# A two-layer diffusion trunk step: the first layer begins by channel blocks, the two empty token columns are dropped, and a gate product stands between each pair of preparation steps

## What is computed

```python
mod = silu(cond) @ w_ada + b_ada                  # cond: c_ctx for context tokens, c for latent tokens
sh1, sc1, g1, sh2, sc2, g2 = split(mod, 6)
h = rms(x, g_norm1) * (1 + sc1) + sh1
u = h @ w_in                                      # 1024 x 5728: 4096 gate columns, then the mixers' inputs
gates, xa, qkv_da, xc, mla_in = split(u)
# four mixers: pooling (xa), differential attention (q, k, v), Fourier (xc), latent attention (cq, ckv)
proj = einsum('btnw,nwd->btnd', branches, w_branch)
x = x + g1 * (sum(sigmoid(gates) * proj) @ w_out)
h2 = rms(x, g_norm2) * (1 + sc2) + sh2
u = h2 @ w_up                                     # 1024 x 5632
u = u[t-1] * conv_w[0] + u[t] * conv_w[1] + u[t+1] * conv_w[2] + conv_b    # within each token group
x = x + g2 * ((silu(gate) * val) @ w_down)        # 2816 x 1024
```

## Time and profile before

| | |
|---|---|
| median of 3 runs | 1329.32 us (1328.96 to 1331.95) |
| the profiled execution, its own time | 1332.93 us |
| its span in the trace | 1331.1 us |
| PE busy | 1290.0 us, 97% of the span |
| DVE busy, ACT busy | 750.8 us (56%), 599.5 us (45%) |
| moved by DMA | 198.05 MB, mean 149 GB/s |
| start of the first stream product | 42.08 us |

### The profile page before, as it was taken

One profiled execution on the slowest core, in us unless ns is written; L12 is line 12 of the kernel. 1 busy time (PEld: TensorE's weight loads), 2 busy tenths in 40 slices (PEclk: granted clock), 3 DMA queues, 4 the chain that ended last, 5 costly groups with the idle time before them and its releaser, 6 DMA issues.

```text
span 1331.1 us, 19314 instructions
## 1 busy us (share of the span) xinstructions
PE 1290.0 (97%) x7808; PEld 1194.1 (90%) x7808; DVE 750.8 (56%) x1292; ACT 599.5 (45%) x1000; POOL 85.3 (6%) x77
## 2 busy tenths in 40 slices
PE   4799999999999999999999999999999999999999
PEld 1796888889989999999989879898899899999998
DVE  0526258544858766673344542874476777777532
ACT  2445555453345544452244554555433655544321
POOL 1000000001810000000000000000053000000000
PEclk9799999999999999999999999999999999999999
DMA  9532144543463444447554312433436333333433
GB/s 365 213 113 88 64 175 143 188 145 123 163 221 112 143 144 153 148 142 258 201 194 162 119 64 73 142 135 133 168 111 222 111 127 127 122 120 123 136 133 127
DMA packets 53544, 198.05 MB, mean 149 GB/s; under 512 B 6416, under 2 KB 6832, under 8 KB 52944
## 3 DMA queue, kind: packets, MB, share of 16 engines
q1 hardware_dynamic: 53136, 196.13, 42.2%
q0 software_dynamic: 320, 0.69, 0.2%
HBM read 194.52 MB, written 2.27 MB: 148 GB/s over the span
## 4 chain that ended last, share of the span: by engine, by line
PE 88%; DVE 5%; issue 2%; SPq 1%; ACT 1%; DMA 1%; POOL 1%; DVEq 0%; POOLq 0%; ACTq 0%
PE bank L1161 25%; PE bank L1163 25%; PE bank L1162 25%; PE bank L1119 2%; PE bank L1373 2%; DVE wide L1035 1%; DMA w_raw<-stream 1%; DVE w_lo L797 1%; PE bank L1403 1%; PE bank L1383 1%; SPq L327 1%; PE bank L1374 1%; PE bank L1347 1%; PE bank L1371 1%; PE bank L1267 0%
## 5 line engine op out<-in xcount | busy, mean ns | idle before, releaser
L1161 PE MATMUL bank<-act_hi,w_hi 128*128 128x386 f32 x1424 | 493.8, 347 | 12.7 <-DVE act_lo L857 12.3
L1163 PE MATMUL bank<-act_hi,w_lo 128*128 128x386 f32 x1424 | 483.0, 339 | 0.0
L1162 PE MATMUL bank<-act_lo,w_hi 128*128 128x386 f32 x1392 | 472.7, 340 | 0.0
L797 DVE TENSOR_TENSOR w_lo<-w_raw,w_hi 128x1024 fp32r<-128x1024 f32 x258 | 317.8, 1232 | 268.8 <-ACT w_hi L489 268.5
L489 ACT ACTIVATE w_hi<-w_raw 128x1024 fp32r<-128x1024 f32 x258 | 270.9, 1051 | 169.0 <-DMA w_raw<-stream 169.0
L1161 PEld LDWEIGHTS bank<-act_hi,w_hi 128*128 128x128 f32 x1424 | 269.8, 189 | 21.3 <-issue 19.8
L1163 PEld LDWEIGHTS bank<-act_hi,w_lo 128*128 128x128 f32 x1424 | 269.5, 189 | 0.0
L1162 PEld LDWEIGHTS bank<-act_lo,w_hi 128*128 128x128 f32 x1392 | 263.9, 190 | 1.3
L1161 PE MATMUL bank<-mlp_hi,w_hi 128*128 128x386 f32 x352 | 120.0, 341 | 0.0
L1162 PE MATMUL bank<-mlp_lo,w_hi 128*128 128x386 f32 x352 | 119.1, 338 | 0.0
L1163 PE MATMUL bank<-mlp_hi,w_lo 128*128 128x386 f32 x352 | 118.9, 338 | 0.0
(11 more groups left out here) (204 smaller groups left out, 1431.6 us busy)
## 6 DMA issues: line engine op xcount, KB each, us to landing
w_raw<-stream SPq DMA_DIRECT2D x258, 512.0 KB, 3.7
ada<-ada_w SPq DMA_DIRECT2D x58, 512.0 KB, 3.7
ada_head_a<-ada_w SPq DMA_DIRECT2D x16, 512.0 KB, 6.3
ada_norm<-ada_w SPq DMA_DIRECT2D x16, 512.0 KB, 5.3
time_consts<-time_consts SPq DMA_DIRECT2D x2, 1920.0 KB, 15.5
ada_head_b<-ada_w SPq DMA_DIRECT2D x6, 512.0 KB, 15.4
params<-params SPq DMA_DIRECT2D x2, 926.0 KB, 11.3
x<-x_in SPq DMA_DIRECT2D x1, 1544.0 KB, 10.6
```

Of the source, the lines that this page charges most:

```text
L797: V.tensor_tensor(wlo[s][:, :], raw[s][:, :], whi[s][:, :].bitcast(F32), ALU.subtract).then_inc(lo_ready, 1)
L1161: T.matmul(out, wb[s][0][:, w, :], hi[k], start=first and k == 0, stop=False)
L1162: T.matmul(out, wb[s][0][:, w, :], lo[k], start=False, stop=False)
L1163: ins = T.matmul(out, wb[s][1][:, w, :], hi[k], start=False, stop=last and k == n - 1)
```

## The change

Three things are changed.

First, GAP is gone: TOK is 384 instead of 386, and everything that was 386 columns wide is 384. The memsets of the empty columns are gone too. Each outer tap of the convolution is made by two instructions, one for each token group (127 and 255 columns), instead of one of 385.

Second, layer 0 begins by channel blocks. w_ada's first two chunks come as 8 blocks of 1 MB, block j with the shift and scale of channel block j only; the first 7 stream units (`SKIP = 7`) come as 8 blocks of 448 KB (128 x 896 numbers), block j with their rows for channel block j. PE makes the modulation of a block with 32 matmuls of 64 moving columns (`start_modulate`) in place of 8 of 256 for the same data, and, when the block's activations are there, the products of that block with all 7 units into 7 banks (`start_products`, 21 matmuls). The squares are shared by ACT and DVE, and PE sums all 8 blocks with 8 matmuls instead of POOL's adds and 3 matmuls. x is loaded first, in two halves.

```diff
-SKIP = 0
+SKIP = 7
...
-MIX = ["xa0", "xa1", "q0", "q1", "k0", "k1", "v0", "v1", "xc0", "xc1", "cq", "ckv", "cqr"]
+MIX = ["xa0", "xa1", "q0", "q1", "k0", "k1", "xc0", "xc1", "v0", "v1", "cq", "ckv", "cqr"]
...
+            for h in range(2):
+                c0, c1 = h * KD // 2 * TOK, (h + 1) * KD // 2 * TOK
+                sp.dma_start(x_t[:, c0:c1], x_in[:, c0:c1]).then_inc(x_loaded[h], 16)
...
+            for j in range(KD):
+                if j >= START_ADA:
+                    sp.wait_ge(ada_done, 2 * (j - START_ADA + 1))
+                sp.dma_start(start_ada_buf[j % START_ADA][:, :], start_ada[j:j + 1, :, :].rearrange("a p n -> (a p) n")
+                             ).then_inc(start_ada_loaded[j % START_ADA], 16)
+                sp.dma_start(start_raw[j][:, :], start_w[j:j + 1, :, :].rearrange("a p n -> (a p) n")
+                             ).then_inc(start_w_loaded[j], 16)
...
+                def start_norm(j):
+
+                    c0 = j * 2 * STRIP
+                    turned_block = rt_t[:, c0:c0 + 2 * STRIP].rearrange("p (b c) -> p b c", c=STRIP)
+                    dve.wait_ge(ada_done, 2 * (j + 1))
+                    turn = V.transpose(rt_t[:, c0:c0 + 2 * STRIP], bank[7][:, c0:c0 + 2 * STRIP])
...
+                    if j == 0:
+                        start_low(0)
+                    own.wait()
+                    dve.wait_ge(rstd_ready, 1)
...
+                def start_squares():
+
+                    for k in range(KD):
+                        if k % 2 == 0:
+                            pe.wait_ge((start_sq_act, start_sq_dve)[k // 2 % 2], k // 4 + 1)
+                        ins = T.matmul(bank[4][:, 0:TOK], cc("ones"), wide[:, k, :], start=k == 0, stop=k == KD - 1)
+                    ins.then_inc(ss_done, 1)
+
+                def start_modulate(j):
+
+                    w = start_ada_buf[j % START_ADA]
+                    pe.wait_ge(start_ada_loaded[j % START_ADA], 16 * (j // START_ADA + 1))
+                    if j >= 1:
+                        pe.wait_ge(start_read, j)
+                    n = 2 * STRIP
+                    for k in range(KD):
+                        for strip in range(4):
+                            p0, c = STRIP * strip, (k * 4 + strip) * n
+                            ins = T.matmul(bank[7][p0:p0 + STRIP, j * n:(j + 1) * n], conds[:, k, :], w[:, c:c + n],
+                                           start=k == 0, stop=k == KD - 1)
+                    ins.then_inc(ada_done, 2)
+
+                def start_products(j):
+
+                    pe.wait_ge(start_w_lo, j + 1)
+                    pe.wait_ge(norm_lo, j + 1)
+                    for u in range(SKIP):
+                        out = bank[u][:, 0:TOK]
+                        wh, wl = start_hi[j][:, u * P:(u + 1) * P], start_lo[j][:, u * P:(u + 1) * P]
+                        T.matmul(out, wh, HI[j], start=j == 0, stop=False)
+                        T.matmul(out, wh, LO[j], start=False, stop=False)
+                        ins = T.matmul(out, wl, HI[j], start=False, stop=j == KD - 1)
...
+                    start_squares()
+                    start_modulate(0)
+                    start_modulate(1)
+                    for j in range(KD):
+                        start_products(j)
+                        if j + 2 < KD:
+                            start_modulate(j + 2)
```

Third, in both layers' preparation a gate product is taken before the first sums of squares, so that gates 0 to 5 stand one step earlier, and the Fourier products come before the pooling products:

```diff
+
+                gate(0)
 
                 pe.wait_ge(mod_read, FROM + 6 * l + 2 + l)
                 pe.wait_ge(psq, l * 7 + 7)
                 T.matmul(bank[6][:, 0:TOK], cc("ones"), wide[:, 4, :], start=True, stop=False)
                 T.matmul(bank[6][:, 0:TOK], cc("ones", 0, NOPE), wide[0:NOPE, 6, :], start=False, stop=True).then_inc(pss, 1)
                 T.matmul(bank[7][:, 0:TOK], cc("ones"), wide[:, 5, :], start=True, stop=True).then_inc(pss, 1)
-                gate(0)
+                gate(1)
...
-                gate(4)
                 gate(5)
```

305 lines of the change are left out of this document (175 added, 130 removed).

## The result

The changed kernel takes a median of 1299.62 us (1297.97 to 1300.75, 4 runs), the kernel before, run beside it, 1329.22. The ratio is 0.9767, with a 95% interval of 0.9752 to 0.9783: 29 to 33 us less. The profiled execution took 1300.75 us with a span of 1299.0, where the one before took 1332.93 with a span of 1331.1.

A forecast was written before the change was run, and what follows sets the result against it. PE, busy 97% of the span, was taken as the bound. Columns 5.7, preparation 4.7 and start 9.8 us sum to 20.2, from the median 1329.3 to 1309 us, with a range of 1301 to 1319.

The forecast's parts named there:

- Term 1: All products: dropping the two empty columns shortens 6,000 matmuls and the float32 sums, 5.7 us in all.
- so two columns less are 0.92 ns: Price of a matmul: 0.46 ns for each column and nothing fixed, read from products of 256 and 386 columns.
- The convolution in two pieces: w_up's taps on DVE: 0.8 us more for two units, covered by DVE's idle 2.2 to 3.0 us; cost 0.
- Term 2: Preparation: gate products placed between its steps cover PE's waits before L1258 and L1267 in both layers, 4.7 us.
- PE waits in three places only: After the start, once a layer: 1.8 us at the merge, 1.2 before L1258, 1.1 before L1267.
- Term 3: Start of layer 0 by channel blocks: seven units through at 64.8 us instead of 74.6, gain 9.8 us, bounds 1 to 18.
- I take 2.1, the middle: Start: modulation of one block, 64 records of 64 columns, put at 2.1 us between bounds of 0.86 and 3.4.
- short matmuls are nearly free: Rival for the start: loads hide and columns decide, start gains 15 to 18 us, 1301 to 1304 us; chance 0.12.
- the bound below: Start: modulation of a block priced by columns alone, 0.86 us; the start would then gain 18 us.
- PE cools in the start: Rival: PE waits about 2 us before product 0, the clock falls, costing 2.4 us, so 1312 us; chance 0.06.
- The merge is not touched: Merge: PE's wait for w_lo, 1.8 us once in a layer, was taken to stay as it is.

The follow-up runs named there:

- e1: Kernel before with only the 384 columns, no gap memsets and the two-piece convolution; old preparation and start: 1319.97 us, ratio 0.9935.
- e4: Changed kernel with 15 rows of 42 products appended, varying width and block stride: 384 columns 173.4 to 175.7 ns, 352 columns 161.2, 400 columns 182.1.
- e9: Kernel before, still 386 columns, with every tile behind act_lo moved up by 384 bytes: 1324.72 us, ratio 0.9961.
- e8: Kernel before, still 386 columns, with every tile behind act_lo moved up by 64 bytes: 1329.46 us, ratio 0.9992.
- e3: Changed kernel with the blocks of the two activation tiles 386 columns apart, products still 384 wide: 1301.10 us, ratio 0.9779.
- e6: Changed kernel with every tile behind act_lo moved up by 128 bytes: 1306.04 us, ratio 0.9801.
- e7: Changed kernel with every tile behind act_lo moved up by 64 bytes: 1299.88 us, ratio 0.9768.
- e14: Changed kernel with every tile behind act_lo moved up by 256 bytes: 1298.35 us, ratio 0.9750.
- e2: Kernel before with 384 columns and the new preparation (a gate product between each pair of steps), old start: 1313.68 us, ratio 0.9871.
- e12: Changed kernel with the start's modulation products of blocks 2 to 7 made twice: 1310.18 us, ratio 0.9847.
- e10: Changed kernel with four float32 products, result unread, filling PE's wait before the start's first product: 1298.19 us, ratio 0.9755.
- e13: Changed kernel with 21 rows of 42 products appended, weights fixed, moving block 0 to 1024 bytes further: 173.1 to 176.9 ns at 384 columns.
- e5: Changed kernel with 21 rows of 42 products appended, moving block and weights at chosen places: 173.3 to 175.7 ns at 384 columns.

## Why the prediction was right or wrong

**Term 1, columns: mis-sized, and the step that put the time outside the range.** 5.7 forecast, 9 (ratio) to 12.7 (traces) measured in e1. The step that failed is "so two columns less are 0.92 ns", which took for granted that a spacing depends on columns alone. The mean spacing of the products on the activations fell by 3.4 ns, from 177.1 to 173.7 (13.8 us over some 4,060 of them), that on the merged blocks by 3.7 ns (1.3 us), and w_down's gave 1.1 us: over 16 us. Of this 2.9 us went into the grown merge waits and some 1 us into the clock, which was low for 10.2 us in e1 behind the start and for 6.8 in before.

The price of a column over a wide span was nearly right (0.44 ns in e4). But the spacing depends on the tiles' places modulo 256 bytes too, and the new width moved all tiles behind the activations. e9 shows 0.95 of the 3.4 ns (3.9 us) by the place alone. The other 2.5 ns came with the width of 384, more than the 0.92 of the columns; why is not shown. With 386 columns each block begins 8 bytes further than the one before, and in the three places tried (before, e8, e9) the mean was 176.2 to 177.4; with 384 it was 173.7 to 176.0 by place (after, e3, e6, e7, e14).

The Trainium skill, page "TensorE: Matmul & The Clock Gate", section "Back-to-back issue gap", gives N/2.4 + 2.5 ns for a matmul by itself at full clock, as an estimate 162.5 ns for 384 columns. No row of 384 columns here is that fast; the lowest is 173.1, 7% more.

The convolution in two pieces cost PE nothing, as forecast: DVE's taps went from 614 to 345 + 474 ns, and PE has no wait in w_up:

```profile
L1138 DVE SCALAR_TENSOR_TENSOR mlp_tmp<-bank,params,mlp_tmp 128x255 f32<-128x255 f32 x88 | 41.7, 474 | 0.0
...
L1138 DVE SCALAR_TENSOR_TENSOR mlp_tmp<-bank,params,mlp_tmp 128x127 f32<-128x127 f32 x88 | 30.4, 345 | 67.7 <-ACT mlp_tmp L511 67.7
```

**Term 2, preparation: right**, 4.7 forecast and 5.7 measured (e1 to e2). The waits went and didn't come back. The waits that went have only 3.8 us in their rows in e1. The other 1.9 are mostly the clock: it fell behind one of these waits in e1's profiled execution, some 1.7 us, and not in e2's. So the 5.7 us are the waits and what the clock cost behind one of them; in how many executions it does is not shown. The prediction's "PE waits in three places only" left out three waits for act_lo behind the start, 1.2 us together (12.3 less 11.1); they are 1.2 us in after too and touch no term.

**Term 3, the start: right in its order, mis-sized in one step, with a rival on top.** Sums done at 16 (15.7), first product at 22.4 (21.1), turns of 5.8 (4.94). The step that failed is "I take 2.1, the middle" for the modulation of a block: it is 0.9 (e12's second block) to 1.2 (a turn less its 21 products). Seven blocks at about 1 us less each are 6 to 7 us, of which the clock took 2.9 back. The rows had an argument for the lower end, the units of 256 columns in which loads cost nothing, and the rival that used it, "short matmuls are nearly free", is what happened. In the trace the records of a block start 7, 7, 6 and 36 ns apart, over and over: the four strips run side by side, and four records of 64 columns cost 56 ns, near the 52 to 54 ns of one record of 256 columns in before, the same number of columns. So it was a price by columns (0.86 forecast as the bound below, 0.9 measured). 1.10 us for 64 records are 17 ns each; the floor of some 25 ns that the same page and section of the Trainium skill state would make it 1.6 us as an estimate, and the trace doesn't agree. "PE cools in the start" happened as well, with the place and nearly the size forecast (2.4 us; idle 2.6 us, 2.9 more than the sum's 3.7 for the 21 products in the profiled execution), and e10 shows it by its removal. That it happened in the profiled execution is in part chance: it did in five of nine. Together: 1.3 us earlier at the first product, 5.2 less in six turns, 2.9 back: 3.6 of the 3.9 us between 64.8 and 60.9. (The sum of the start comes to 64.6 and not 64.5, and its lower bound to 8.7 us cheaper and not 8.5, for seven blocks and not eight; neither changes the forecast.)

**"The merge is not touched": wrong.** It is touched by the columns. The chain from merged block to merged block in the kernel after, POOL's last round and what stands behind it:

```profile
333.71 1.93 POOL L504 TENSOR_TENSOR merge_sum<-wide 128x384 f32<-128x384 f32 x1
...
335.67 0.52 ACT L511 ACTIVATE merged_hi<-merge_sum 128x384 fp32r<-128x384 f32 x1 [2.81 <-POOL merge_sum L504]
...
336.11 1.04 ACT L511 ACTIVATE w_hi<-w_raw 128x1024 fp32r<-128x1024 f32 x1
...
337.18 1.77 DVE L828 TENSOR_TENSOR w_lo<-w_raw,w_hi 128x1024 fp32r<-128x1024 f32 x1 [1.12 <-ACT w_hi L511]
```

POOL sets the pace here with three operations a block, and each round takes 4.28 us where it took 4.15, though it has fewer columns: merge_sum went from 1.02 to 1.93 us, the first addition from 1.79 to 1.34, the second from 1.18 to 1.01. What changed is which of them starts just behind DVE's weight split w_lo. In before it is the first addition, and merge_sum runs ahead of the split:

```profile
347.10 1.02 POOL L482 TENSOR_TENSOR merge_sum<-wide 128x386 f32<-128x386 f32 x1
348.09 1.21 DVE L797 TENSOR_TENSOR w_lo<-w_raw,w_hi 128x1024 fp32r<-128x1024 f32 x1
348.24 1.79 POOL L479 TENSOR_TENSOR wide<-wide 128x386 f32<-128x386 f32 x1
```

In after it is merge_sum itself, 333.71 behind this split:

```profile
333.55 1.21 DVE L828 TENSOR_TENSOR w_lo<-w_raw,w_hi 128x1024 fp32r<-128x1024 f32 x1
```

The operation in that place lasts some 0.9 us longer in both. ACT and then the split for the output stage wait for merge_sum. Against the start of the branch products the last merge_sum ahead of that split ends 2.1 us later than before (352.29 - 319.42 and 335.64 - 300.71): five longer rounds are 1.0 us of it, its own length 0.9. PE's own branch products became only 0.2 us shorter (319.42 to 354.85 before, 300.71 to 335.94 after), so a faster PE isn't the reason. 0.7 us were covered, since before ACT's high part lay ready that long ahead of DVE, and DVE's last split is 0.1 us shorter (1.89 and 1.77). That leaves the 1.4 us by which the wait grew in each layer. e9, with 386 columns, has the old wait. That POOL's operation is held up by DVE's is a reading of these rows, which no run varied by itself, and why two columns less change the order is open.

**The sum.** Forecast 20.2; by the ratios 31: columns 9, preparation 8 (5.7 in the traces), start 14; e9's spacing puts the tiles' place at 4 of the first. The sign was sure. The rival "short matmuls are nearly free" alone gave 1301 to 1304, inside the range; below 1301 the time came by term 1, whose bounds the range left out. No row of before varied the place, since all its products of one width had nearly one spacing. That the miss is only 1.4 us is partly luck: in the profiled execution the merge's longer waits (2.9 us) and the clock in the start (2.9) took back some 6 us of what the two prices had left out.

## What to carry to other kernels

Where one operation is most of the span, a spacing read at one place isn't its price everywhere: a change of tile length moves every tile behind it, so compare the spacing by stage first, and try pads below 256 bytes ahead of the weights; here they moved a kernel of 1300 to 1330 us by up to 6 us either way. A wait of an engine that idles at its end costs more than its row if its clock can fall; filling 2.6 us with products that nobody reads kept it up. When two profiled executions are compared, look where the clock fell in each: of the 6.8 us between before and e9 more than 3, and of the 5.7 us between e1 and e2 1.7, were that. A split queued behind a late hand-over waits with it; put it one block earlier.

## What the runs showed of the hardware

- The spacing of gapless products of 384 columns repeats every 256 bytes of the moving block's place: 173.3 ns at 0 and 64 bytes, 175.7 and 176.9 at 128 and 192, 173.8 at 256 (e13). 386 columns stand at 176.4 to 176.7 there, yet at 173.3 with the block 8 bytes further (e5). Why w_down changed in e6 while weights and block kept their distance, and why the same tiles of w_down took 173.6 ns with nothing beside them (e5) and 176.7 in the kernel, stays open.
- Matmuls of 64 columns in four strips start 7, 7, 6 and 36 ns apart, 17 ns a record on average (1.10 us for 64).
- After PE idled 2.6 us in the start the granted clock fell in five of nine traces (after, e6, e7, e12, e14; not in e3, e4, e5, e13), and the 21 products behind it took 5.4 to 6.6 us instead of 3.9; at the merge a wait of 3.3 us did the same in some layers and not in others, and in before one of 1.8 us did, where 1.7 us in e9 didn't. Much of the spread of one kernel's times goes with the clock: e6's at 1306 have 0.994 to 0.995, those at 1301.6 0.998; e1's two high ones 0.986, the others 0.990 to 0.992.
- An operation of two inputs of 384 columns on POOL takes between 1.0 and 2.0 us, one of 386 between 0.87 and 1.9. In the rounds of the merge above, the long one is the one that starts just behind a weight split on DVE.
